# A decoder layer on one core: the low weights of every fourth chunk are computed by GpSimd instead of VectorE

## The reference

```
h = rmsnorm(x)
b, c, xt, v = split(h @ w_in)                       # 2048 x 4096
y_conv = b * causal_depthwise_conv3(c * xt)
y_pool = scale * group_linear(trailing_mean(v) - v) # windows 2, 4, 8, 16
x = x + concat(y_conv, y_pool) @ w_out              # 2048 x 2048
x = x + relu(rmsnorm(x) @ w_up)**2 @ w_down         # 2048 x 8192, 8192 x 2048
return rmsnorm(x)
```

## Time and profile before

| | us |
|---|---|
| median of three runs | 1000.58 |
| the profiled execution | 1000.99 |
| its span in the trace | 999.2 |
| TensorE busy in the span | 986.5 |
| VectorE busy | 586.4 |
| ScalarE busy | 419.6 |
| GpSimd busy | 1.4 |

### The profile page before, as it was taken

One profiled execution on the slowest core, in us unless ns is written; L12 is line 12 of the kernel. 1 busy time (PEld: TensorE's weight loads), 2 busy tenths in 40 slices (PEclk: granted clock), 3 DMA queues, 4 the chain that ended last, 5 costly groups with the idle time before them and its releaser, 6 DMA issues.

```text
span 999.2 us, 12457 instructions
## 1 busy us (share of the span) xinstructions
PE 986.5 (99%) x5088; PEld 847.2 (85%) x5088; DVE 586.4 (59%) x428; ACT 419.6 (42%) x325; POOL 1.4 (0%) x9
## 2 busy tenths in 40 slices
PE   8999999999999999999999999999999999999996
PEld 7888888888888888888888888888888888888885
DVE  6597777655554766544656654556565445656453
ACT  6644435354443434333444433343433334444342
POOL 0000000000000000000000000000000000000000
PEclk9999999999999999999999999999999999999998
DMA  9956543555544655555455455545545554555512
GB/s 327 392 194 229 190 188 122 215 211 190 189 169 169 233 189 195 183 208 177 165 211 206 176 203 191 187 151 213 209 183 207 176 204 132 211 209 205 187 66 84
DMA packets 29694, 193.52 MB, mean 194 GB/s; under 512 B 3296, under 2 KB 3552, under 8 KB 7136
## 3 DMA queue, kind: packets, MB, share of 16 engines
q1 hardware_dynamic: 29232, 190.85, 52.1%
q10 hardware_dynamic: 288, 1.18, 0.3%
q0 software_dynamic: 144, 1.05, 0.3%
HBM read 190.97 MB, written 2.10 MB: 193 GB/s over the span
## 4 chain that ended last, share of the span: by engine, by line
PE 94%; DMA 3%; SPq 1%; DVE 1%; ACT 0%; issue 0%; ACTq 0%
PE ps L343 44%; PE ps L252 33%; PE ps L255 17%; DMA w_raw<-w_stream 3%; SPq L208 1%; PE ps L277 0%; PE ps L329 0%; SPq L193 0%; DVE w_lo L628 0%; ACT w_hi L449 0%; PE ps L317 0%; DVE val L635 0%; PE ps L276 0%; PE ps L279 0%; ACT cross L483 0%
## 5 line engine op out<-in xcount | busy, mean ns | idle before, releaser
L628 DVE TENSOR_TENSOR w_lo<-w_raw,w_hi 128x2048 fp32r<-128x2048 f32 x172 | 392.0, 2291 | 280.4 <-ACT w_hi L449 279.7
L449 ACT ACTIVATE w_hi<-w_raw 128x2048 fp32r<-128x2048 f32 x172 | 326.8, 1912 | 344.0 <-PE ps L343 210.8
L252 PE MATMUL ps<-act_a,w_hi 128*128 128x512 f32 x1472 | 351.1, 391 | 0.0
L343 PE MATMUL ps<-w_hi,act_b 128*128 128x512 f32 x1280 | 345.3, 390 | 0.0
L252 PEld LDWEIGHTS ps<-act_a,w_hi 128*128 128x128 f32 x1472 | 271.0, 188 | 52.5
L343 PEld LDWEIGHTS ps<-w_hi,act_b 128*128 128x128 f32 x1280 | 239.8, 188 | 49.3
L343 PE MATMUL ps<-w_lo,act_b 128*128 128x512 f32 x640 | 199.7, 389 | 0.0
L255 PEld LDWEIGHTS ps<-act_a,w_lo 128*128 128x128 f32 x1472 | 188.6, 191 | 7.0
L255 PE MATMUL ps<-act_a,w_lo 128*128 128x256 f32 x1472 | 191.1, 283 | 0.0
L343 PEld LDWEIGHTS ps<-w_lo,act_b 128*128 128x128 f32 x640 | 120.2, 188 | 25.0
L635 DVE TENSOR_TENSOR val<-ps,cross 128x1024 f32<-128x1024 f32 x26 | 31.8, 1223 | 47.2 <-ACT cross L455 47.2
(11 more groups left out here) (68 smaller groups left out, 164.3 us busy)
## 6 DMA issues: line engine op xcount, KB each, us to landing
w_raw<-w_stream SPq DMA_DIRECT2D x172, 1024.0 KB, 4.8
w_raw<-w_stream SPq DMA_DIRECT2D x16, 256.0 KB, 7.9
x<-x_rows SPq DMA_DIRECT2D x2, 1024.0 KB, 17.4
mix_mem<-x_t SPq DMA_DIRECT2D x3, 512.0 KB, 8.2
out<-x SPq DMA_DIRECT2D x6, 256.0 KB, 2.7
mix_mem<-pool_w ACTq DMA_DIRECT2D x1, 1024.0 KB, 9.1
mix_mem<-g_final POOLq DMA_DIRECT2D x1, 1024.0 KB, 5.0
out<-val SPq DMA_DIRECT2D x2, 256.0 KB, 2.1
```

Of the source, the lines that this page charges most:

```text
L252: return pe.matmul(ps[:, bank, :], weights_hi, act, start=first, stop=False)
L343: mm = pe.matmul(ps[:, NT * parity + t, :], a[:, at:at + P], cols, start=first and i == 0, stop=last and i == 2)
L449: act.activation(w_hi[:, c, :], w_raw[:, c, :], ACT.Copy).then_inc(hi_ready, 1)
L628: dve.tensor_tensor(out=w_lo[:, c, :], in0=w_raw[:, c, :], in1=w_hi[:, c, :].bitcast(F32), op=ALU.subtract)\
```

## The change

Chunk 3 of every block from 1 to 43 is subtracted by GpSimd, into the same w_lo from the same w_raw and w_hi. It counts on a semaphore of its own, lo_last; the pieces of block 0's chunk 3 stay on VectorE and raise lo_first at the end; lo_ready now counts three chunks per block. All who waited for lo_ready (SyncE before a load, TensorE before the products) go through wait_lo, which picks the semaphore by the chunk.

```diff
+        def wait_lo(engine, n, c):
+
+            if c == CHUNKS - 1 and isinstance(n, int) and n == 0:
+                engine.wait_ge(lo_first, 1)
+            elif c == CHUNKS - 1:
+                engine.wait_ge(lo_last, n)
+            else:
+                engine.wait_ge(lo_ready, (CHUNKS - 1) * n + (c + 1))
...
             def load_chunk(n, c):
-                sp.wait_ge(lo_ready, 4 * n + (c - 3))
+                wait_lo(sp, n - 1, c)
...
             pool.memset(win[:, :, :, 0:PAD], 0.0).then_inc(consts_set, 1)
+            def lo_of_last(n):
+
+                pool.wait_ge(hi_ready, 4 * n + 4)
+                pool.tensor_tensor(out=w_lo[:, 3, :], in0=w_raw[:, 3, :], in1=w_hi[:, 3, :].bitcast(F32),
+                                   op=ALU.subtract).then_inc(lo_last, 1)
+
             pool.wait_ge(x_lo_ready, KT)
             pool.memset(v[:, :, 0:PAD], 0.0).then_inc(v_pads_zero, 1)
+            lo_of_last(1)
             pool.wait_ge(pool_w_ready, 1)
             pool.memset(u[:, :, 0:2], 0.0).then_inc(u_pads_zero, 1)
-
+            for n in range(2, FIRST_OUT + 1):
+                lo_of_last(n)
             pool.wait_ge(value_ready, 2)
             pool.dma_start(g_row, g_final[0:1, :].to_broadcast([P, D])).then_inc(g_loaded, 16)
+            for n in range(FIRST_OUT + 1, BLOCKS):
+                lo_of_last(n)
...
-                    pe.wait_ge(lo_ready, 4 * n + (c + 1))
+                    wait_lo(pe, n, c)
...
         def _(dve):
             def split(n, c):
 
+                if c == CHUNKS - 1:
+                    return
                 dve.wait_ge(hi_ready, 4 * n + (c + 1))
```

More of the change, by code:

```diff
@@ L113, in build @@
         lo_ready = sem("lo_ready")
+        lo_first = sem("lo_first")
+        lo_last = sem("lo_last")
         chunk_used = sem("chunk_used")
@@ L379, in _ @@
                 if is_last(k):
-                    pe.wait_ge(lo_ready, k // CK + 1)
+                    wait_lo(pe, 0, k // CK)
                 else:
@@ L433, in _ @@
                         pe.wait_ge(act_ready, 4 * PARTS + 4 + (c + 1))
-                        pe.wait_ge(lo_ready, 4 * (BLOCKS - 1) + (c + 1))
+                        wait_lo(pe, BLOCKS - 1, c)
                     for k in range(CK):
@@ L722, in _ @@
                     dve.wait_ge(piece_hi, k - k // CK + 1)
-                dve.tensor_tensor(out=w_lo[:, k // CK, piece(k)], in0=w_raw[:, k // CK, piece(k)],
-                                  in1=w_hi[:, k // CK, piece(k)].bitcast(F32), op=ALU.subtract)\
-                   .then_inc(lo_ready if is_last(k) else piece_lo, 1)
+                op = dve.tensor_tensor(out=w_lo[:, k // CK, piece(k)], in0=w_raw[:, k // CK, piece(k)],
+                                       in1=w_hi[:, k // CK, piece(k)].bitcast(F32), op=ALU.subtract)
+                if k == KT - 1:
+                    op.then_inc(lo_first, 1)
+                else:
+                    op.then_inc(lo_ready if is_last(k) else piece_lo, 1)
             for c in range(CHUNKS):
```

## The result

The changed kernel takes 1004.01 us (median of seven runs, 1003.06 to 1005.57); the kernel before 1000.58 (seven runs, 1000.02 to 1002.70). The ratio is 1.0031, interval 1.0019 to 1.0043: slower by 3.4 us, where 1.1 us less was forecast. The profiled execution took 1005.57 us, with a span of 1003.5.

What follows compares the result with a forecast made beforehand. TensorE was taken to bound the kernel (986.5 us busy of a 999.2 span), with one wait of 1.54 us to shorten. The median 1000.58 less a gain of 1.12 gave 999.5 us, range 998.9 to 1004.2.

Steps and rivals of the forecast that it cites:

- From the root to TensorE's restart: Block 1's norm: the stretch from ScalarE's root to TensorE going on, 2.90 us, taken to stay the same after the change.
- little or no mutual blocking: The forecast's own case: GpSimd and VectorE hardly hold each other off, time 999.5 us; chance 0.48.
- Rival 1: Block 1: GpSimd's first subtraction blocks the tiny products of VectorE's norm chain, restart 2.7 us later, 1003.2 us; chance 0.28.
- The 5.5 us of the forecast: Assumed length of one GpSimd subtraction of 2048 elements, as three passes priced from its constant fills; range 1.9 to 5.5.
- The clock: An allowance of 1 us in the range for a fall of the granted clock in a TensorE gap of 4.2 us.
- VectorE's 98.5 us: Busy time of the 43 subtractions of 2.29 us taken from VectorE, said to buy nothing by itself.
- The gain of 1.12 us on the chain: Block 1: TensorE's one wait falls from 1.54 to 0.42 us, with restart at 46.94 instead of 48.06.
- The table load was late next: Block 1: with the mean ready before 43 us, ScalarE's table load sets the root's start, about 44.04, 1.12 us earlier.
- the tightest: Last block: w_hi ready at 971.30, chunk 3 due at 977.5, leaving 6.1 us for GpSimd's subtraction; met by 0.6 us.
- The chain of the three products there: Last block: under rival 1's rule (Rival 1), three VectorE products would run from 976.85 to 980.3, hidden behind TensorE's products.
- Rivals 2 and 3: 2: VectorE stretches GpSimd's subtractions, 1010 us, chance 0.13. 3: the subtraction alone exceeds the bound, 1011 at 10 us, chance 0.05.

Runs made afterwards that it cites:

- e7: The changed kernel with GpSimd's first subtraction (block 1's chunk 3) cut into 8 instructions of 256 columns: 1003.53 us, ratio 1.0031 to the kernel before.
- e1: The changed kernel with GpSimd's first subtraction held back until VectorE has written both parts of diag: 999.15 us against 1000.41 for the kernel before.
- e3: The kernel before with only block 1's chunk 3 subtracted by GpSimd, the other 42 on VectorE: 1003.68 us, ratio 1.0027.
- e5: The kernel before with two unused sums on VectorE ahead of block 1's norm, lengthening TensorE's wait without GpSimd: 1003.46 us against 1000.51.
- e2: The changed kernel with block 1's chunk 3 subtracted by VectorE again, the other 42 on GpSimd: 1000.73 us against 1000.41 for the kernel before.
- e8: The kernel before with the norm's spreading moved on TensorE behind block 1's chunk 3 instead of chunk 2: 998.62 us, ratio 0.9982.
- e9: The changed kernel with the norm chain's products and constant step done one column at a time, each diag as 127 columns and one: 1001.84 us against 1000.58.
- e4: The changed kernel with the norm chain's three products as one-column tensor_scalars, each with one tensor operand: 1003.60 us, ratio 1.0027 to the kernel before.

## Why the prediction was wrong

**The step that failed** is a term of the sum: "From the root to TensorE's restart it is 48.06 - 45.16 = 2.90 us", taken over unchanged, with GpSimd's effect on VectorE's chain put at nothing. The stretch measured 49.78 - 44.09 = 5.69 us. The difference is the first product, 2.96 us instead of 0.16; with its 2.80 us more the forecast's path comes to 44.09 + 2.90 + 2.80 = 49.79. Behind it stands the choice among the cases: "Forecast, with little or no mutual blocking: 0.48", against 0.28 for the rival that happened. The argument against that rival was that "a blocked 128x2 operation would be an all-or-nothing rule". It is one: the operation waits for the end of GpSimd's instruction (the product of the kernel after until 47.49 for 47.47; in e7 each link for one piece), and with the two kept apart it takes 0.16 us (e1).

The page of the Trainium skill that the text cites beside the rival, SBUF — State Buffer (section Who interferes with whom), says that a VectorE instruction with two SBUF inputs contends with a GpSimd instruction that reads SBUF; the product of the kernel after agrees, held for 2.80 us. It was given too little weight against a trace that had no case of it: GpSimd had read nothing in it.

**Rival 1 held, with its size.** Its rule was that the first product waits for GpSimd's end and that TensorE restarts 2.46 us after the product starts to run. With the 4.6 us that the subtraction took, that is 42.86 + 4.61 + 2.46 = 49.93 us; measured 49.78. The 5.5 us of the forecast gave 50.72. The page GPSIMD Engine Reference of the Trainium skill (section 3.1, Elementwise, side-by-side cycle accounting) came nearer with its 4497 ns; measured here are 4.61 us.

**The clock was named and not priced.** The range had 1 us for it. The profiled execution lost 2.6 us to it. Over the medians an estimate is 3.43 - 1.72 = 1.7 us, the 1.72 being the later restart in the one profiled execution; not all executions lose the same (e3's twelve lie between 1000.92 and 1004.88 us). e5 shows that it hangs on the wait and not on GpSimd. The median, 1004.0, was inside the range (998.9 to 1004.2), but at its end, and not by the forecast's account.

**What held.** VectorE's 98.5 us were worth nothing by themselves (e2). The gain of 1.12 us on the chain was there once the hold was gone (e1: 1.3 us by the medians, 1.0 by TensorE's restart at 47.03 for 48.06). The table load was late next: the root starts at 44.09 where 44.04 was forecast. Every w_lo was in time, the tightest too: in the last block GpSimd ended at 975.74 + 4.62 = 980.4, and chunk 3 was due at about 981.8 (the 977.5 of the forecast, later by what was lost in block 1). The chain of the three products there was held (one of them 4.46 us instead of 1.21) and hidden, as worked out. In block 8 it is VectorE that waited, not GpSimd: its two subtractions from 209.47 take 7.12 us, where they took 4.49. Rivals 2 and 3 fall: GpSimd's subtractions are 4.61 to 4.64 us in 41 of 43 places, overlapped or not, and 5.11 and 5.12 us in two.

**Not settled:** which forms and widths exactly make VectorE wait. Of tensor_scalars, 1 column was seen free, and 2, 127 and 256 columns held; why the reciprocal of 128x2 runs free was not tried. Nor why e7's profiled execution kept its clock after 3.2 us of wait while the changed kernel's lost it after 3.2.

## What to carry to other kernels

Before work goes to GpSimd, look not at the busy shares but at what VectorE does in the same microseconds: a short chain of tiny operations that TensorE waits for is the wrong neighbour, since a link of two values can wait for a whole instruction of GpSimd. Cutting GpSimd's instruction into 8 did not help this chain (e7); ordering it behind the chain did (e1). And a wait of the bounding engine that is already there is the place to look first: giving TensorE its next products in place of the wait was one number, and worth 1.9 us (e8), where 98 us of work taken from VectorE were worth nothing measurable.

## What the runs showed of the hardware that was not expected

- When a VectorE operation with two operands in SBUF is first, GpSimd waits. Two subtractions of the kernel after start while such a one runs, and last 5.11 and 5.12 us instead of 4.6. The first of them:

```profile
107.49 1.23 DVE L687 TENSOR_TENSOR mix_mem<-val,inv_rms 128x1024 f32<-128x1024 f32 x1
108.75 5.52 DVE L835 TENSOR_TENSOR mix_mem<-mix_mem,inv_rms 128x1024 f32<-128x1024 f32 x1
```

```profile
108.08 5.11 POOL L254 TENSOR_TENSOR w_lo<-w_raw,w_hi 128x2048 fp32r<-128x2048 f32 x1 [17.50 <-ACT w_hi L470]
```

  The product of 107.49 keeps its 1.23 us, GpSimd's instruction is longer by some 0.5, and the next product, at 108.75, is held for 4.3 us. In both places who started first kept going.
- A sum of VectorE with one operand in PSUM and one in SBUF is not held, and does not hold GpSimd. In the kernel after one starts inside GpSimd's subtraction of 158.50 to 163.14 and lasts 1.23 us, as alone; in e1 one is first, at 45.76, GpSimd starts at 46.00 within it, and both keep their 1.22 and 4.60 us:

```profile
159.43 1.23 DVE L658 TENSOR_TENSOR val<-ps,cross 128x1024 f32<-128x1024 f32 x1 [1.04 <-ACT cross L476]
```

- The clock after a wait of TensorE: 1.5 us (the kernel before) and 2.7 us (e9) left it at 1.00 from 50 to 56 us; 3.2 us lowered it in the changed kernel (0.54) and in e4 (0.82), not in e7 (1.00); 3.3 us (e3) and 3.9 us (e5) lowered it (0.72 in both).
